# Eight experts with a token list each: three single-pass products of split weights replaced by fp32 products in four 32-column strips, issued strip by strip

## The reference

```python
logits = (xt @ w_router).astype(jnp.float32)
top_v, top_i = lax.top_k(logits, TOP_K)          # TOP_K = 2, N_EXPERTS = 8
top_w = jax.nn.softmax(top_v, axis=-1)
gates = jnp.sum(jax.nn.one_hot(top_i, N_EXPERTS) * top_w[..., None], axis=1)
for e in range(N_EXPERTS):
    h = xt @ w_gu[e]                             # 1024 x 5632
    y = (jax.nn.silu(h[:, :D_EXPERT]) * h[:, D_EXPERT:]) @ w_down[e]   # 2816 x 1024
    out = out + gates[:, e:e + 1] * y
```

## Time and profile before

| | |
|---|---|
| time, median of 2 runs | 1269.26 us (1268.96 to 1269.56) |
| span of the profiled execution | 1267.7 us |
| PE busy | 1242.9 us, 98% |
| DVE, ACT busy | 1003.8 us, 834.6 us |
| expert stage on PE | 503.4 to 1252.2 us |
| DMA in the expert stage | 382 to 393 GB/s |

### The profile page before, as it was taken

One profiled execution on the slowest core, in us unless ns is written; L12 is line 12 of the kernel. 1 busy time (PEld: TensorE's weight loads), 2 busy tenths in 40 slices (PEclk: granted clock), 3 DMA queues, 4 the chain that ended last, 5 costly groups with the idle time before them and its releaser, 6 DMA issues.

```text
span 1267.7 us, 16828 instructions
## 1 busy us (share of the span) xinstructions
PE 1242.9 (98%) x6731; PEld 1060.1 (84%) x6731; DVE 1003.8 (79%) x868; ACT 834.6 (66%) x842; POOL 101.7 (8%) x120
## 2 busy tenths in 40 slices
PE   9999999999999999999999999999999999999995
PEld 8998998888888978888888888888888888888884
DVE  6877846556646677988888888888888988898897
ACT  6795344545534474777777777777777777778773
POOL 4044212000001001300000000000000000001100
PEclk9999999999999999999999999999999999999998
DMA  9834013997554514999999999999999999999991
GB/s 315 271 148 137 2 34 125 413 348 243 181 186 163 192 43 166 333 397 397 389 393 389 390 384 371 391 388 372 389 387 377 386 391 378 382 380 363 390 397 74
DMA packets 189060, 375.75 MB, mean 296 GB/s; under 512 B 12321, under 2 KB 69777, under 8 KB 188977
## 3 DMA queue, kind: packets, MB, share of 16 engines
q1 hardware_dynamic: 179888, 345.02, 75.1%
q0 software_dynamic: 6928, 25.82, 5.4%
q10 hardware_dynamic: 2160, 3.79, 0.8%
HBM read 354.13 MB, written 20.45 MB: 295 GB/s over the span
## 4 chain that ended last, share of the span: by engine, by line
PE 88%; DMA 5%; DVE 3%; ACT 2%; POOL 1%; issue 1%; SPq 0%; DVEq 0%; POOLq 0%; ACTq 0%
PE ps L1529 85%; DMA raw<-in_ffn_w_gu 2%; DMA raw<-in_moe_w_gu 2%; PE ps L2041 1%; ACT hi L572 1%; DVE lo L946 1%; ACT ps L587 0%; PE ps L2034 0%; PE ps L1887 0%; PE ps L1660 0%; DMA x<-in_x 0%; DVE xT_both L954 0%; POOL lnrs L425 0%; SPq L306 0%; DVE x L1502 0%
## 5 line engine op out<-in xcount | busy, mean ns | idle before, releaser
L946 DVE TENSOR_TENSOR lo<-raw,hi 128x2048 fp32r<-128x2048 f32 x326 | 744.9, 2297 | 183.0 <-ACT hi L572 182.0
L572 ACT ACTIVATE hi<-raw 128x2048 fp32r<-128x2048 f32 x326 | 625.5, 1919 | 298.1 <-PE ps L1529 260.7
L1529 PE MATMUL ps<-hi,xg_hi 128*128 128x512 f32 x704 | 278.0, 395 | 0.1
L1529 PE MATMUL ps<-hi,xg_lo 128*128 128x512 f32 x704 | 274.6, 390 | 0.0
L1529 PE MATMUL ps<-lo,xg_hi 128*128 128x512 f32 x704 | 274.2, 389 | 0.0
L1529 PE MATMUL ps<-xT_both,hi 128*128 128x256 f32 (+1 forms) x896 | 222.9, 328 | 4.4 <-DVE xT_both L954 2.5
L1529 PE MATMUL ps<-xT_both,lo 128*128 128x256 f32 x624 | 175.8, 282 | 0.0
L1529 PEld LDWEIGHTS ps<-xT_both,hi 128*128 128x128 f32 x896 | 151.4, 191 | 20.1 <-issue 2.9
L1529 PEld LDWEIGHTS ps<-hi,xg_hi 128*128 128x128 f32 x704 | 132.2, 188 | 28.7 <-DVE lo L946 1.5
L1529 PEld LDWEIGHTS ps<-hi,xg_lo 128*128 128x128 f32 x704 | 132.1, 188 | 28.1
L1529 PEld LDWEIGHTS ps<-lo,xg_hi 128*128 128x128 f32 x704 | 132.3, 188 | 26.4
(11 more groups left out here) (315 smaller groups left out, 1249.3 us busy)
## 6 DMA issues: line engine op xcount, KB each, us to landing
raw<-in_moe_w_gu SPq DMA_DIRECT2D x352, 512.0 KB, 7.2
raw<-in_moe_w_down SPq DMA_DIRECT2D x176, 512.0 KB, 7.1
raw<-in_ffn_w_gu SPq DMA_DIRECT2D x44, 512.0 KB, 8.1
raw<-in_dn_w_in SPq DMA_DIRECT2D x32, 512.0 KB, 8.9
raw<-in_ffn_w_down SPq DMA_DIRECT2D x22, 512.0 KB, 4.0
xe<-xTf POOLq DMA_DIRECT2D x1, 8192.0 KB, 29.0
raw<-in_dn_w_out SPq DMA_DIRECT2D x8, 512.0 KB, 3.9
ys<-xTf POOLq DMA_DIRECT2D x1, 4096.0 KB, 40.3
```

Of the source, the lines that this page charges most:

```text
L572: act.activation(slot(hi, j), slot(raw, j), ACT.Copy).then_inc(hi_ready, 1)
L946: dve.tensor_tensor(slot(lo, j), slot(raw, j), slot(hi, j).bitcast(F32), ALU.subtract).then_inc(lo_ready, 1)
L1529: return pe.matmul(dst, lhsT, rhs, start=start, stop=stop)
```

## The change

The expert stage alone is changed, and the tables that it needs.

- Nothing is split. PE multiplies fp32 tokens (`xgT`) and fp32 hidden values (`hE`) by the loaded weights.
- An expert has room for 96 tokens, three groups of 32. The stationary operand is 32 columns wide (one group) and the output goes to 32 partitions: quarter `j` of the array, here called a strip, takes quarter `j` of the unit's output columns. A unit of gate and up is one eighth of the contraction with 1024 columns of gate and as many of up (the last eight units of an expert: 768 of each). It holds 24 matmuls of 256 (192) columns: for each of the four strips the six products of three groups by gate and up. A unit of the way down holds 24 matmuls of 256 columns, twice (for two pieces of the contraction) three groups on each of four strips. All are in the order of the loops in `products` and `expert`: all of strip 0, then all of strip 1, and so on.
- The units are 35 for an expert (24 of gate and up, 11 down), with the same bytes as the 33 before. The ring is of 13 units: the 6 of `raw`, 6 in the place of `hi` and `lo`, and one more. SP refills a place when PE has used it.
- Hidden values and gathered tokens are turned by DVE in blocks of 32x32; PE's transposes are gone.
- The table `xe` is cleared after layer 0's last norm, with 9.4 MB, where 8.4 MB of it and 5.2 MB of `ys` were cleared at the start of the dense SwiGLU. Of `ys` one row is cleared.
- An overflow of 96 would run two more passes. It isn't taken either.

```diff
-    CHUNKS = FF // 512 + 1
-    GU_E = 4 * (CHUNKS - 1) + 2
+    WIDTHS = (D, D, FF - 2 * D)
+    CHUNKS = len(WIDTHS)
+    GU_E = KD * CHUNKS
     PER_E = GU_E + FC
+    GROUPS = 3
+    CAP = 32 * GROUPS
+    RING = RAW + 2 * CUT + 1
...
+            def expert_unit(n, e, it=None, p=0):
...
+                elif n < RAW:
+                    sp_.wait_ge(lo_ready, U_MOE - RAW + n + 1)
+                elif n < RING:
+                    sp_.wait_ge(unit_used, U_O + 1 + min((n - RAW) // 2, CUT - 1) + 1)
                 else:
+                    sp_.wait_ge(unit_used, done(n - RING))
...
-            zeros = xTf[:, 0:4, :].rearrange("p k t -> p (k t)").unsqueeze(1)
-            pool.dma_start(xe.rearrange("(r s) d -> s r d", s=P), zeros.to_broadcast([P, 2 * E, D])).then_inc(xe_clear, 16)
-            pool.dma_start(ys_v[1].rearrange("e s d -> s e d"), zeros.to_broadcast([P, E, D])).then_inc(ys_clear, 16)
...
             norm(1)
+            rows = E * (1 + LATE) * CAP // P
+            pool.dma_start(xe.rearrange("(k r) d -> r k d", r=P), zeros.unsqueeze(1).to_broadcast([P, rows, D])).then_inc(xe_clear, 16)
...
+            def turn_xg(s, q):
+                dve.wait_ge(gathered, 64 * s)
+                spaced = turned_act(0, actE[:, q, :])
+                dve.tensor_copy(spaced.rearrange("p g t b -> p g b t"),
+                                xg[:, :, :].rearrange("p g (b t) -> p g b t", t=KD)).then_inc(xg_spaced, 1)
+                dve.wait_ge(xg_spaced, s)
+                dve.transpose(xgT[:, :, :, :].rearrange("p g t r -> p (g t r)"), actE[:, q, :]).then_inc(xg_here, 1)
+
+            def hidden(s, c, n, it=None, p=0):
...
+                dve.tensor_tensor(turned_act(c, actE[:, q, :]).rearrange("p g t b -> p g b t"),
+                                  sgE[:, q, 0:n_].rearrange("p (g b t) -> p g b t", g=GROUPS, b=32),
+                                  up.rearrange("p g (b t) -> p g b t", b=32), ALU.mult).then_inc(act_here, 1)
+                dve.wait_ge(act_here, CHUNKS * s + c + 1)
+                dve.transpose(hE[:, c, 0:n_], actE[:, q, 0:n_]).then_inc(h_here, 1)
...
-                                for kk in range(4):
-                                    k = 4 * a + kk
-                                    mm(dst, xg_hi[:, k, :], w_hi[:, kk, :], k == 0, False)
-                                    mm(dst, xg_hi[:, k, :], w_lo[:, kk, :], False, False)
-                                    last = mm(dst, xg_lo[:, k, :], w_hi[:, kk, :], False, k == KD - 1)
-                                last.then_inc(unit_used, 1)
...
+            def products(w, c, t, k):
+                n_ = WIDTHS[c] // 4
+                for j in range(4):
+                    for i in range(2 * GROUPS):
+                        r = slice(32 * j, 32 * j + 32)
+                        col = D * (i // GROUPS) + n_ * j
+                        last = mm(ps[r, 3 * (k % 2) + i // 2, 256 * (i % 2):256 * (i % 2) + n_], xgT[:, i % GROUPS, t, :],
+                                  w[:, col:col + n_], t == 0 and i % 2 == 0, t == KD - 1 and i % 2 == 1)
+                return last
+
+            def down(w, c, t, kk, g, quarters=range(4)):
+                h = turned_act(c, hE[:, c, :])
...
+                for j in quarters:
+                    r = slice(32 * j, 32 * j + 32)
+                    col = D * kk + 256 * j
+                    last = mm(ps[r, 6 + g // 2, 256 * (g % 2):256 * (g % 2) + 256], h[:, g, t, :], w[:, col:col + 256],
+                              first and g % 2 == 0, final and g >= 1)
+                return last
+
+            def expert(s, n0, q, y_clear, it=None, p=0):
...
+                        products(w, c, t, q + c).then_inc(unit_used, 1)
...
+                    for kk in range(2):
+                        for j in range(4):
+                            for g in range(GROUPS):
+                                last = down(w, c, 2 * u + kk, kk, g, (j,))
+                    last.then_inc(unit_used, 1)
```

More of the change, by code:

```diff
@@ L353, in store @@
+            for n in range(FAST):
+                expert_unit(n, n // PER_E)
             def store(i):
@@ L363, in _ @@
             full = sp_.value_load(cint[0:1, 0:1], min_val=0, max_val=T)
[L364 removed]
+            with sp_.If(full > CAP):
                 sp_.wait_ge(out_done, 48)
[L366 removed]
+                sp_.wait_ge(unit_used, done(FAST - 1))
+                for p in range(LATE):
+                    with sp_.Fori(0, TURNS) as it:
+                        for n in range(PER_IT):
+                            expert_unit(n, 2 * it + n // PER_E, it, p)
                 store(4)
@@ new lines, in _ @@
+            route_gates()
+            for s in range(E):
+                if s:
+                    turn_xg(s, s % 2)
+                for c in range(CHUNKS):
+                    hidden(s, c, PER_E * s + KD * c + KD - 1)
+            for b in range(NB):
+                for i in range(2):
+                    add_picked(b, i)
+            full = dve.value_load(cint[0:1, 0:1], min_val=0, max_val=T)
+            dve.wait_ge(y_there, 64 * (E - 1))
+            dve.wait_ge(unit_used, done(FAST - 1))
@@ L1515, in _ @@
+            norm(3, None, None, add_spread)
+            with dve.If(full > CAP):
+                for p in range(LATE):
+                    with dve.Fori(0, TURNS) as it:
+                        for b in range(2):
+                            s = late_pass(it, p, b)
+                            turn_xg(s, b)
+                            for c in range(CHUNKS):
+                                hidden(s, c, PER_E * b + KD * c + KD - 1, it, p)
                 for b in range(NB):
@@ new lines, in _ @@
+            for s in range(E):
+                expert(s, PER_E * s, s, s + 1)
+            full = pe.value_load(cint[0:1, 0:1], min_val=0, max_val=T)
+            busy(1, 0)
+            for b in range(NB):
+                for m in range(GROUPS):
+                    if b == 0 and m == 0:
+                        pe.wait_ge(y7_act, 1)
+                    if b == 0 and m == 2:
+                        pe.wait_ge(y7_dve, 1)
+                    for j in range(4):
+                        r = slice(32 * j, 32 * j + 32)
+                        last = mm(ps[:, 4 * b + j, 0:256], onehT[r, b, m, :], ysb[r, m, :], m == 0, m == GROUPS - 1)
+                last.then_inc(spread, 1)
@@ L2127 @@
+            with pe.If(full > CAP):
+                pe.wait_ge(spread_added, NB)
+                for p in range(LATE):
+                    with pe.Fori(0, TURNS) as it:
+                        for b in range(2):
+                            s = late_pass(it, p, b)
+                            expert(s, PER_E * b, b, s, it, p)
 _INS = ["x", "dn_w_in", "dn_conv_w", "dn_a_log", "dn_dt_bias", "dn_norm_w", "dn_w_out", "w_kv_shared", "sw_w_q",
```

602 lines of the change are left out of this document (245 added, 357 removed).

## The result

The changed kernel takes 2107.29 us (median of 2 runs, 2106.5 to 2108.08) against 1269.26 us: 1.661 times the time before (95% interval 1.658 to 1.665). The prediction was slower, 1828 us, with a range up to 2060; the time lies 2% above the range.

A forecast was written before the change was run, and what follows sets the result against it. PE's list in the expert stage was taken as the bound: with five records held per strip, eight experts take 1310 us, plus 517.5 us outside the stage, 1828 us in all; range 1190 to 2060 us.

The forecast's parts named there:

- DMA share near half: Sign of the forecast being right: in the expert stage, DMA about half used during gate and up, SP waiting for PE.
- 5.2 us for both: Sign in the expert stage: units of gate and up and units down both at 5.2 us mean two strips served at once.
- 8 to 9 us for both: Sign in the expert stage: both kinds of unit at 8 to 9 us mean records start in list order.
- h: Expert stage: records a strip holds, running one included; 4 to 6, taken as 5, giving 6.15 us per gate and up unit.
- room enough: Clearing moved to 420 to 460 us, where DMA is busy 0.45 and 0.32: 24 us of DMA fit without cost.
- The 3 us that come back: Dense SwiGLU: with the clearing gone from 217 us, PE regains 16 matmuls or 3 us (0 to 5).
- under 1 us each way: Gather and tail around the expert stage: 32 records of 96 columns for 128 change the time by under 1 us.
- All strips work: Rival, expert stage: a common pool or at least 9 places per strip, nearly fourfold overlap, 1198 to 1205 us; chance 0.19.
- Two at a time: Rival, expert stage: only two strips served at once, every unit 24 slots, whole 1881 us; chance 0.08.
- hardly any overlap: Rival, expert stage: list order, only a strip's last record coincides with the next strip's first, 2941 us; chance 0.05.
- the queue of 64: PE's queue, from the skill: 64 deep with partial reorder window, so 32 records in view and nearly all the fourfold had.
- the second group of values: Attention's values: four records of one half listed before the other's take 0.67 us, so records are set aside, at least three.

The follow-up runs named there:

- the first three experiments: The changed kernel with strips taking turns of one matmul, of two, then of three for gate and up with 12 records down: 1244.87, 1246.56, 1815.53 us.
- the first experiment: The changed kernel with one matmul (2 records) of a strip at a time, loops over strips innermost: 1244.87 us, 0.982 of the kernel before.

## Why the prediction was wrong

**What held.** That the order of the list decides, and that overlap ends where a strip's places are full: shown by the first three experiments. PE as the bound, with DVE and ACT far from it; the list itself (48 records in a unit, 35 units); the record, 0.215 taken and 0.216 measured; loads of 32 columns hidden; DMA as the next bound near 690 us. The list of signs had "DMA share near half" (0.51 to 0.57 measured). Its "5.2 us for both" and "8 to 9 us for both" are refuted.

**The step that failed: h.** The prediction's step was the number h of records that a strip holds. It bounded h by 4 from below, out of the values of the attention, and from above by 5 places behind the running record, as 17 matmuls before a semaphore less some 12 in the common queue; it read 4 to 6 and took the middle, h = 5. It is 4 exactly. The lower bound was a count of records that did coincide; the upper one a difference of two roundings from a reading of queues, and it deserved no weight beside the first. The middle of a range is no evidence.

**The sum, term by term.** The time is 279 us above the forecast.

| term | predicted | measured | us |
|---|---|---|---|
| unit of gate and up, 256 columns, x128 | 6.15 us | 7.03 | +113 |
| the same, 192 columns, x64 | 4.63 us | 5.32 | +44 |
| unit down, x88 | 2.58 us | 3.69 | +98 |
| start and rest of the stage | 0 | 3.5 | +3.5 |
| everything outside the stage | 517.5 us | 538.8 | +21 |

The first two are h alone: 32.6 slots and not 28.6, and 32.6 is what the prediction gave for h = 4. The third is h and one thing more. For h = 4 the prediction has 8 slots for half a unit down, 3.44 us; measured are 8.54. Its formula for gate and up carried 0.6 slots for four changes of strip, the 0.03 us each that the timeline shows (609.39 to 609.42); the number for the way down left them out, 0.25 us a unit or 22 us in all. This and the 21 us outside the stage are most of why even the time for h = 4, 2054, is 53 us low. The range ended at that time, as if everything else in it were exact; it should have had the other terms' errors on top.

**Outside the stage: "room enough".** The 3 us that come back in the dense SwiGLU came: the 1100 records from PE's 1500th on take 191.2 us before and 187.4 after, 3.8 less. But DMA's idle share at 420 to 460 us was the wrong view. The clearing ran from 405 to 444 us and not from 420 on, and took 38.8 us and not 24, since the weights had their part of the 420 GB/s. That cost nothing by itself: behind the sinks' load it took 43.3 us, and the kernel was 17 us faster. What hurt was one DMA of 8 KB that POOL issues next on the same queue, 35.5 us and not 4.6 to its landing, and DVE's list behind it. The prediction said "if it were not, it would cost no more than those 24", and that bound held, at 17, for another reason than DMA's rate; the central value, nothing, ignored who stands on the queue behind the moved DMA. The Trainium skill (DMA: Bandwidth & Descriptors, "Two DMAs through the same engine are not ordered") says that within one queue of one DMA engine descriptors start in order; by it a small load behind a large one starts when the large one has nearly gone, and the 35.5 and 3.6 us of these runs agree. The other 4 us are the one-hot product, forecast at "under 1 us each way": its tokens are read with a stride, and its loads take 335 ns for 192.

**Rivals.** *All strips work* is wrong for this order and right for another: 1198 to 1205 were worked out for it, 1227.8 measured once the order is mended. *Two at a time* and *hardly any overlap* fell with the first experiment, which has four strips at work. The prediction took the queue of 64 as a window in which matmuls pass each other, for the first rival. The Trainium skill (TensorE: Matmul & The Clock Gate, Part 2, "Step-by-step: what each phase is for") has the reorder for weight loads alone and the matmuls in program order, so the page gave that rival no support. And where the prediction argues from the second group of values, strict order with one coincidence makes 6 steps, 0.93 us, and not 7 steps and 1.04; the 0.67 us of the earlier trace rows lie below both, so the conclusion stands. The Trainium skill's rule that matmuls run "strict FIFO, no reordering" (TensorE: Matmul & The Clock Gate, Part 3, "What overlaps and what doesn't") doesn't fit these runs: at 609.39 to 609.83 us three records start that stand ahead, in the list, of the one that started at 609.18. By the rule a unit of gate and up would take 44 slots or 9.46 us; it took 7.03.

## What to carry to other kernels

When a matmul uses part of the array, write the list so that neighbours go to different parts, and let no part have more than 4 records in a row (two fp32 matmuls, four one-pass ones); beyond that a round of n records on each of s strips costs about s x (n - 4) slots where that is more than n, and a busy TensorE at 98% won't tell. Read overlap from starts per microsecond, not from busy time. When a large DMA is moved, look at what is issued behind it on its own queue before looking at bandwidth.

## What the runs showed of the hardware

- A part of the array (a strip of 32 or 64 columns, or half the rows) holds 4 records, and a full one stops the whole list. Four strips of fp32 matmuls start a record every 54.0 ns in turns of up to 4, 76.9 in turns of 6 and 146.4 in turns of 12.
- The four places are each part's own, not common to all: 24 records in turns of 6 take 8.54 slots, and four strips begin within 0.04 us while three records wait in the first.
- Changing the strip costs 0.03 us with 32 columns, 0.06 with 64 and 0.11 with halves of rows, when the turn is long.
- Records of 64 moving columns in four strips start every 14.0 ns.
- A weight load of 128 fp32 columns that reads every eighth number takes 335 ns, 192 when they lie side by side, and a matmul record of 96 columns then waits for it: 0.24 us apart at either clock.
- 8 KB behind 9.4 MB on POOL's queue land after 35.5 us; ahead of them after 3.6.
